# Three layer norms: half of the elementwise work moved from VectorE to ScalarE and GpSimd

## The reference, cut to what matters

```python
def _layer_norm(x, g, b):
    xf = x.astype(jnp.float32)
    mu = jnp.mean(xf, axis=-1, keepdims=True)
    var = jnp.mean(jnp.square(xf - mu), axis=-1, keepdims=True)
    y = (xf - mu) * lax.rsqrt(var + LN_EPS)
    return (y * g.astype(jnp.float32) + b.astype(jnp.float32)).astype(x.dtype)

x = first_block(x, ...)                     # ends with rms_norm(x, final_norm)
x = _layer_norm(x, ln_emb_g, ln_emb_b)      # norm 0
...                                         # proj = x @ w_in, attention, recurrence
x = _layer_norm(DEEPNORM_ALPHA * x + mix, ln_mix_g[l], ln_mix_b[l])   # norm 1
...                                         # up projection, convolution, gelu, down projection
x = _layer_norm(DEEPNORM_ALPHA * x + ffn, ln_ffn_g[l], ln_ffn_b[l])   # norm 2, the output
```

## Time and profile before

| | |
|---|---|
| median of 3 runs | 1375.38 us (1373.71 to 1377.1) |
| the profiled execution's own time | 1378.31 us |
| its span, first to last instruction | 1376.5 us |
| granted TensorE clock over the span | 0.98 |
| instructions | 19597 |

### The profile page before, as it was taken

One profiled execution on the slowest core, in us unless ns is written; L12 is line 12 of the kernel. 1 busy time (PEld: TensorE's weight loads), 2 busy tenths in 40 slices (PEclk: granted clock), 3 DMA queues, 4 the chain that ended last, 5 costly groups with the idle time before them and its releaser, 6 DMA issues.

```text
span 1376.5 us, 19597 instructions
## 1 busy us (share of the span) xinstructions
PE 1317.0 (96%) x7417; PEld 1143.1 (83%) x7417; DVE 954.6 (69%) x1272; ACT 729.9 (53%) x996; POOL 156.0 (11%) x136
## 2 busy tenths in 40 slices
PE   7999999699999999999999999999988999899996
PEld 6888887588888888888898888888888987788884
DVE  5766666868766676666667676666768678687777
ACT  6544456765444455444557755444454443465662
POOL 1200002258300000000025310000004110000000
PEclk9999999799999999999999999999998999999998
DMA  7755544046665546565454266555523343365650
GB/s 243 247 189 183 186 151 151 31 136 189 216 198 185 185 154 213 190 198 189 153 168 139 93 211 208 199 192 183 153 92 111 103 154 123 128 208 184 208 187 31
DMA packets 165425, 229.24 MB, mean 167 GB/s; under 512 B 4027, under 2 KB 135354, under 8 KB 165248
## 3 DMA queue, kind: packets, MB, share of 16 engines
q1 hardware_dynamic: 163120, 221.33, 49.3%
q0 software_dynamic: 2160, 7.24, 1.8%
q10 hardware_dynamic: 96, 0.02, 0.0%
HBM read 227.52 MB, written 1.05 MB: 166 GB/s over the span
## 4 chain that ended last, share of the span: by engine, by line
PE 83%; DVE 10%; ACT 3%; issue 2%; POOL 1%; DMA 0%; ACTq 0%; DVEq 0%
PE ps L425 28%; PE ps L432 15%; PE ps L371 12%; PE ps L372 11%; PE ps L373 11%; DVE w_lo L304 2%; POOL p_sb L1423 1%; PE ps L1336 1%; PE ps L639 1%; PE ps L2159 1%; ACT w_hi L296 1%; DVE h_both L675 1%; PE ps L1299 0%; DMA pt_sb<-in_ffn_norm_dram 0%; ACT h_both L658 0%
## 5 line engine op out<-in xcount | busy, mean ns | idle before, releaser
L304 DVE TENSOR_TENSOR w_lo<-raw,w_hi 128x2048 fp32r<-128x2048 f32 x208 | 479.8, 2308 | 110.8 <-ACT w_hi L296 110.7
L425 PE MATMUL ps<-h_both,w_hi 128*128 128x512 f32 x1760 | 424.9, 392 | 5.9 <-DVE h_both L770 2.9
L296 ACT ACTIVATE w_hi<-raw 128x2048 fp32r<-128x2048 f32 x208 | 396.5, 1908 | 15.4 <-PE ps L373 15.4
L425 PEld LDWEIGHTS ps<-h_both,w_hi 128*128 128x128 f32 x1760 | 326.4, 189 | 72.3 <-DVE w_lo L324 2.2
L432 PEld LDWEIGHTS ps<-h_both,w_lo 128*128 128x128 f32 x1760 | 228.3, 192 | 9.6
L432 PE MATMUL ps<-h_both,w_lo 128*128 128x256 f32 x1760 | 231.7, 283 | 0.0
L855 ACT ACTIVATE s_sb<-ps 128x512 f32<-128x512 f32 x88 | 52.5, 597 | 230.9 <-PE ps L432 230.9
L371 PE MATMUL ps<-w_hi,gu_hi 128*128 128x512 f32 x400 | 156.4, 391 | 0.8 <-DVE w_lo L304 0.8
L372 PE MATMUL ps<-w_hi,gu_lo 128*128 128x512 f32 x400 | 156.2, 391 | 0.0
L373 PE MATMUL ps<-w_lo,gu_hi 128*128 128x512 f32 x400 | 155.6, 389 | 0.0
L861 DVE TENSOR_TENSOR s_sb<-ps,s_sb 128x512 f32<-128x512 f32 x88 | 60.8, 690 | 103.4 <-ACT s_sb L855 103.4
(11 more groups left out here) (334 smaller groups left out, 1688.5 us busy)
## 6 DMA issues: line engine op xcount, KB each, us to landing
raw<-in_ffn_w_up_dram SPq DMA_DIRECT2D x44, 1024.0 KB, 5.3
raw<-in_ffn_w_down_dram SPq DMA_DIRECT2D x44, 1024.0 KB, 4.9
raw<-in_ffn_w_gate_dram SPq DMA_DIRECT2D x43, 1024.0 KB, 5.3
raw<-in_w_up_dram SPq DMA_DIRECT2D x22, 1024.0 KB, 5.0
raw<-in_w_in_dram SPq DMA_DIRECT2D x14, 1024.0 KB, 5.3
raw<-in_odd_w_qkv_dram SPq DMA_DIRECT2D x12, 1024.0 KB, 5.1
raw<-in_w_down_dram SPq DMA_DIRECT2D x11, 1024.0 KB, 4.9
raw<-in_even_w_in_dram SPq DMA_DIRECT2D x4, 1024.0 KB, 5.2
```

Of the source, the lines that this page charges most:

```text
L296: act.activation(w_hi[slot][:, :], raw[slot][:, :], ACT.Copy).then_inc(w_hi_ready, 1)
L304: dve.tensor_tensor(w_lo[slot][:, :], raw[slot][:, :], w_hi[slot][:, :].bitcast(F32), ALU.subtract).then_inc(w_lo_ready, 1)
L425: pe.matmul(PS[:, bank, :], a[:, k, t * P:(t + 1) * P], h_both[:, :, k, :], start=k == 0, stop=False, skip_group_check=True)
```

## The change

In all three layer norms the quarters of the upper feature half (quarters 2 and 3) lose VectorE's first instruction. In its place VectorE writes the negated mean to a new tile, neg_mean, right after the statistics are joined (`dve_mean`). ScalarE then adds neg_mean to each of the two upper quarters in place (`act_centre`), and GpSimd multiplies each by the weight row in place (`pool_gain`). VectorE takes the root meanwhile, does quarters 0 and 1 with its two instructions each as before, and for quarters 2 and 3 waits on the semaphore gained and does only the second instruction. In norm 0 the two engines work in XN and VectorE's second instruction reads XN.

The three semaphores for the arrival of the rows become one, vec_in, with waits for 48, 80 and 112. The transfers themselves and their order stay as they were.

```diff
--- before.py
+++ after.py
@@ -165,6 +165,7 @@
         gcol = sb("gcol", [P, 6 * KC])
         rs_tok = sb("rs_tok", [P, TB])
         rs_half = sb("rs_half", [P, TB])
+        neg_mean = sb("neg_mean", [P, TB])
         rs_wide = nc.alloc_sbuf_tensor_at("rs_wide", [P, S], F32, offset=place["fox_k_lo"])
         PS = ctx.enter_context(nc.psum_tensor("ps", [P, 8, 512], F32))
 
@@ -1828,6 +1829,28 @@
                 dve.bn_stats(bn[:, tb, half, :], X[:, tb, half * 512:(half + 1) * 512]).then_inc(stats_done, 1)
             return stats
 
+        mean_ready = sem("mean_ready")
+        centred = sem("centred")
+        gained = sem("gained")
+        upper = slice(512, 1024)
+
+        def dve_mean(dve):
+
+            dve.tensor_scalar(neg_mean[:, :], mv[:, :, 0], -1.0, None, ALU.mult).then_inc(mean_ready, 1)
+
+        def act_centre(act, at, z):
+
+            act.wait_ge(mean_ready, at + 1)
+            for tb in range(TB):
+                act.activation(z[:, tb, upper], z[:, tb, upper], ACT.Identity, bias=neg_mean[:, tb:tb + 1])\
+                   .then_inc(centred, 1)
+
+        def pool_gain(pool, at, z, g):
+
+            for tb in range(TB):
+                pool.wait_ge(centred, 2 * at + tb + 1)
+                pool.tensor_tensor(z[:, tb, upper], z[:, tb, upper], g[:, upper], ALU.mult).then_inc(gained, 1)
+
         def layer_norm(dve, at, g, b, rows_in, done, norm=None):
 
 
@@ -1835,13 +1858,17 @@
             for tb in range(TB):
                 m = dve.bn_aggr(mv[:, tb, :], bn[:, tb, :, :].rearrange("p a b -> p (a b)"))
             dlink(dve, m)
+            dve_mean(dve)
             dlink(dve, dve.tensor_scalar(ss[:, 0:2], mv[:, :, 1], EPS_LN, None, ALU.add))
             rsqrt(dve, ss[:, 0:2], 2)
-            dve.wait_ge(rows_in, 32)
+            dve.wait_ge(vec_in, rows_in)
             for tb, half in QUARTERS:
                 f = slice(half * 512, (half + 1) * 512)
                 x = X[:, tb, f]
-                dlink(dve, dve.scalar_tensor_tensor(x, x, mv[:, tb, 0:1], g[:, f], ALU.subtract, ALU.mult))
+                if half == 0:
+                    dlink(dve, dve.scalar_tensor_tensor(x, x, mv[:, tb, 0:1], g[:, f], ALU.subtract, ALU.mult))
+                else:
+                    dve.wait_ge(gained, 2 * at + tb + 1)
                 dve.scalar_tensor_tensor(x, x, ss[:, tb:tb + 1], b[:, f], ALU.mult, ALU.add).then_inc(done, 1)
                 if norm is not None and tb == 1:
                     norm.dve(dve, half=half)
@@ -1885,8 +1913,12 @@
                 for tb, half in QUARTERS:
                     f = slice(half * 512, (half + 1) * 512)
                     x = X[:, tb, f]
-                    dlink(dve, dve.scalar_tensor_tensor(x, XN[:, tb, f], mv[:, tb, 0:1], g[:, f], ALU.subtract, ALU.mult))
-                    dve.scalar_tensor_tensor(x, x, ss[:, tb:tb + 1], b[:, f], ALU.mult, ALU.add).then_inc(done, 1)
+                    if half == 0:
+                        dlink(dve, dve.scalar_tensor_tensor(x, XN[:, tb, f], mv[:, tb, 0:1], g[:, f], ALU.subtract, ALU.mult))
+                    else:
+                        dve.wait_ge(gained, tb + 1)
+                    z = x if half == 0 else XN[:, tb, f]
+                    dve.scalar_tensor_tensor(x, z, ss[:, tb:tb + 1], b[:, f], ALU.mult, ALU.add).then_inc(done, 1)
                     if tb == 1:
                         norm.dve(dve, half=half)
 
@@ -2443,8 +2475,6 @@
         bias_in = sem("bias_in")
         bias_masked = sem("bias_masked")
         vec_in = sem("vec_in")
-        vec2_in = sem("vec2_in")
-        vec3_in = sem("vec3_in")
         out_stored = sem("out_stored")
 
         g_rows_in = sem("g_rows_in")
@@ -2554,18 +2584,23 @@
 
             fox.pool_zero(pool)
             fox.pool_wf(pool)
+            pool.wait_ge(vec_in, 48)
+            pool_gain(pool, 0, XN, rowvec[:, 1, :])
             rec.pool(pool)
 
             pool.wait_ge(att_fox.scores, 8)
-            pool.dma_start(rowvec[:, 1, :], io["ln_mix_b_2"][0].partition_broadcast(P)).then_inc(vec2_in, 16)
+            pool.dma_start(rowvec[:, 1, :], io["ln_mix_b_2"][0].partition_broadcast(P)).then_inc(vec_in, 16)
             rec_out.pool(pool)
 
             pool.wait_ge(att_fox.out_ready, 8)
-            pool.dma_start(rowvec[:, 0, :], io["ln_mix_g_2"][0].partition_broadcast(P)).then_inc(vec2_in, 16)
+            pool.dma_start(rowvec[:, 0, :], io["ln_mix_g_2"][0].partition_broadcast(P)).then_inc(vec_in, 16)
+            pool.wait_ge(vec_in, 80)
+            pool_gain(pool, 1, X, rowvec[:, 0, :])
             pool.wait_ge(n_conv.normed, 3 * 4)
-            pool.dma_start(rowvec[:, 0, :], io["ln_ffn_g_2"][0].partition_broadcast(P)).then_inc(vec3_in, 16)
-            pool.dma_start(rowvec[:, 1, :], io["ln_ffn_b_2"][0].partition_broadcast(P)).then_inc(vec3_in, 16)
-            pool.wait_ge(vec3_in, 32)
+            pool.dma_start(rowvec[:, 0, :], io["ln_ffn_g_2"][0].partition_broadcast(P)).then_inc(vec_in, 16)
+            pool.dma_start(rowvec[:, 1, :], io["ln_ffn_b_2"][0].partition_broadcast(P)).then_inc(vec_in, 16)
+            pool.wait_ge(vec_in, 112)
+            pool_gain(pool, 2, X, rowvec[:, 0, :])
 
         @block.scalar
         def _(act):
@@ -2620,6 +2655,7 @@
             ffn2_1.act(act)
             fox.act_wf(act)
             final_norms.act(act)
+            act_centre(act, 0, XN)
             n_emb.act(act)
             for what, n in REC:
                 if what in ("unit", "second"):
@@ -2650,8 +2686,10 @@
                     n_gated.act(act, half=n)
                 elif what == "rec_proj":
                     rec_proj.act(act, n)
+            act_centre(act, 1, X)
             n_conv.act(act)
             conv_ffn.act(act)
+            act_centre(act, 2, X)
 
         @block.vector
         def _(dve):
@@ -2745,9 +2783,9 @@
                     n_gated.dve(dve, half=n)
                 elif what == "rec_proj":
                     rec_proj.dve(dve, n, stats_of(dve, mixed_x))
-            layer_norm(dve, 1, rowvec[:, 0, :], rowvec[:, 1, :], vec2_in, n_conv.normed, n_conv)
+            layer_norm(dve, 1, rowvec[:, 0, :], rowvec[:, 1, :], 80, n_conv.normed, n_conv)
             conv_ffn.dve(dve, stats_of(dve, conv_x))
-            layer_norm(dve, 2, rowvec[:, 0, :], rowvec[:, 1, :], vec3_in, out_x)
+            layer_norm(dve, 2, rowvec[:, 0, :], rowvec[:, 1, :], 112, out_x)
 
         @block.tensor
         def _(pe):
```

## The result

The changed kernel is slower: a median of 1384.8 us (1376.87 to 1386.69, five runs) against 1375.01 (1371.05 to 1377.1, five runs) for the kernel before, a ratio of 1.0061 with a 95% interval of 1.0039 to 1.0083. It was timed again twelve times beside 35 runs of before (e1_after_again): 1384.26 against 1375.49, ratio 1.0048 (1.0034 to 1.0063). The forecast was 1380.8, with a range to 1383.0.

The account below looks back on a forecast made before the run. TensorE, in flight for 96% of the span, was taken as the bound, norm work counting only where it waits. Norms of + 2.3, + 2.3 and + 0.8 made + 5.4 us on the median 1375.38: 1380.8 us, range 1377.0 to 1383.0.

Parts of the forecast that it names:

- VectorE stands until GpSimd's instruction is over.: Root in each norm: VectorE's small steps wait out GpSimd's two multiplies; 2.3 us a norm, bounds 0 and 2.8.
- (3): Rival, root in all norms: the tiny instructions slip past the two multiplies; - 1.2 us, 1374.2; chance 0.15.
- (5): Rival, on top of (3): earlier upper quarters speed TensorE in norms 0 and 1; - 4.3 us, 1371.1; chance 0.03.
- Norms 0 and 1 save nothing: Quarters 2 and 3 there have 1.4 us of slack ahead of TensorE, so dropping VectorE's first instructions brings nothing.
- the wait on gained never ends last: Norm 2: the multiplies end by 1369.63, and quarter 2 asks no sooner than 1371.11, so VectorE is not delayed.
- Norm 2.: Last norm: + 2.3 for the stopped root, - 1.56 saved, + 0.1 for store overlap, together + 0.8 us.
- The sum of the three norms.: Norm 0 + 2.3, norm 1 + 2.3, norm 2 + 0.8, together + 5.4 us; as the forecast, chance 0.50.
- In the sum I keep this cost as it is.: TensorE's restart: the half-rate stretch of 6.1 us, seen at norm 0, was taken to cost the same after the change.
- That execution lies 2.9 us above the median, so I put the difference on the median.: Whole kernel: + 5.4 was added to the median 1375.38, giving 1380.8, not to the profiled execution, which would give 1383.7.
- (2): Rival, restarts of norms 0 and 1: the clock returns at the same moment, giving 1.15 us back each; 1378.5; chance 0.20.
- (4): Rival, restarts: the slow stretch grows too, + 7.7 us, or the quarters also stand behind a late multiply; 1383.1; chance 0.12.

Follow-up runs that it names:

- e2: The changed kernel without GpSimd's multiplies, VectorE waiting on ScalarE's centring instead (part of the computation left out); 1372.86 us, ratio 0.998.
- e7: The changed kernel with only token block 0's upper quarter moved, so one GpSimd multiply a norm; 1379.68 us, ratio 1.0024.
- e8: The changed kernel with GpSimd clearing 1400 elements of a scratch tile in place of each multiply; 1369.52 us in one run.
- e10: The changed kernel with GpSimd's multiplies in norms 0 and 1 waiting until quarter 1 is written; 1374.90 us, ratio 1.0001.
- e12: The changed kernel with the root's products in PSUM and its estimate kept in both SBUF and PSUM; 1380.60 us, ratio 1.0039.
- e4: The kernel before plus eleven linked small VectorE steps ahead of the root in norms 0 and 1; 1382.46 us, ratio 1.0039.
- e5: The changed kernel with ten more filler matmuls ahead of the first turn in each of norms 0 and 1; 1381.36 us, ratio 1.0037.
- e14: The changed kernel with both the longer first fills of e5 and the seven fillers of e6; 1377.04 us, ratio 1.0014.
- e6: The kernel before plus seven filler matmuls around TensorE's turns in each of norms 0 and 1; 1371.16 us, ratio 0.9969.
- e11: The changed kernel with the root's scratch in PSUM, done column by column, eighteen small steps instead of nine; 1382.59 us, ratio 1.0065.

## Why the prediction was too low

- *VectorE stands until GpSimd's instruction is over.* Right. Taken as 2.3 us a norm; 2.09, 2.10 and 2.05 measured. Two long steps a norm, of 1.1 to 1.2 us, on the lines that it named (each one line further down in the new kernel). e2, e7, e8 and e10 show that it is the multiplies, that it goes by their number, and, with one run of e8 beside e12, that it takes two inputs of VectorE in SBUF and a GpSimd instruction that reads it. Rivals (3) and (5), with no stop, are out. The rows that it was read from were thinner than the text says: in the earlier trace rows the small steps start 0.68 and 0.66 us apart, not 0.65, and an addition takes 0.85 on the average.
- *Norms 0 and 1 save nothing; the wait on gained never ends last.* Right: both quarters 2 and 3 follow each other with no idle time (1005.04, 1.40 for the pair), and TensorE's restart moved by the delay of quarter 0 (0.18 us more in norm 1, from a turn at the lower clock).
- *Norm 2.* Forecast + 0.8, the trace shows + 0.6; of that the saving was 1.56 and measured 1.57.
- *The sum of the three norms.* Forecast + 5.4, the traces show + 4.8, and the means less the clock's part + 4.3.
- *"In the sum I keep this cost as it is."* This is the step that failed: the change in the clock's cost was put at nothing, and it measured + 3.8 us (an estimate, from 11 us more at the lower level). The rows that it rested on the earlier trace rows came from an execution in which the clock fell at both restarts, at norm 0 to a window mean of 0.89; kernels with an equally early restart read 0.94 and 1.00 in other executions. Held back by about 2 us, norm 0 reads 0.89 in all four profiles. e4 shows that a delay alone brings more time at the lower level (7.7 us, standard error 2.9), e5 that closing the gap undoes it on the average, e14 that with the clock held the loss is the fixed part.
- *"That execution lies 2.9 us above the median, so I put the difference on the median."* The same mistake once more. That execution had a mean clock of 0.980 against 0.9836 for the mean of 107, 10 us more at the lower level, which at 0.34 is 3.4 us and so all of the 2.9. The changed kernel has such a clock, or a lower one, in 13 of 17 runs. Added to its own execution the sum gave 1383.7, near the medians of 1384.8 and 1384.3, but by luck: nothing in the prediction said that the changed kernel would run at that execution's clock.
- *Rivals (2) and (4).* (2), that the clock gives part back, has the wrong sign. (4), that the slow stretch grows too, was right in kind and near in size, + 7.7 for a measured + 8.0 in the means; it had 0.12. The size is partly luck: it took 1.15 us of longer slow stretch at each restart, on top of a fall taken as given, where the runs show a fall that comes in more of the executions.

What is not settled: why the time at the lower level differs so much in the recurrence behind norm 0. Single profiles there read 0.94 to 1.00 (1020 to 1160 us) for late and early restarts alike. Of the 25 us at the lower level that lie between the two profiles of the changed kernel (mean clocks 0.987 and 0.978), about 14 are there (1.00 against 0.95) and 3 in the window of norm 1. So the restarts alone don't explain the spread of its runs, and one or two profiles for each kernel are too few to say whether a late restart bears on the recurrence.

## What to carry to other kernels

Before work is moved to GpSimd, list what VectorE runs in that time, and how much of it takes two inputs from SBUF: each GpSimd instruction that reads SBUF can hold up one such instruction for nearly its whole length, however small that one is (here 0.16 us of work, 1.1 to 1.2 us of standing). Put the moved work where the chain has slack (e10, which loses nothing but gains nothing either), not where the two engines seem to share the time best. And where TensorE's restart hangs on a chain of another engine, price a delay there by many runs with their granted clocks: a profile tells what one execution's clock did, and a few filler matmuls around the restart (e6) can be worth more than the change under study.

## What the runs showed of the hardware

- A VectorE step of 128 x 2 elements with two inputs in SBUF stood for 1.1 to 1.2 us under a GpSimd multiply of 1.25 us; the same step with one of the two in PSUM took 0.17 (e12), two steps of 128 x 1 that read PSUM alone took 0.36 together (e11), and a 128 x 512 one with an input in PSUM took its 0.69 (e10). Under GpSimd's clears all took 0.16 (e8). The Trainium skill, SBUF — State Buffer, section "Who interferes with whom", says this in full: one input in SBUF outside the two-port modes doesn't contend, two do, and only with a GpSimd instruction that reads. These runs agree on both kinds of input and on the reading. They didn't try a small step with a single input in SBUF and none in PSUM under a multiply; the one row of that kind, the start value L588 in the earlier trace rows, took 0.62 us under GpSimd's additions, and why is not shown.
- When the small steps slip past, the next instruction with two inputs in SBUF meets the rest of the multiply (e12's 1.64 us for 0.75).
- The same kernel's runs differ by up to 9 us (before, 1370.6 to 1379.8), in step with their mean granted clock of 0.989 to 0.980 (3.3 us for 10 us more at the lower level). Kernels whose restarts come about 2.1 us later spend 8 to 11 us more at the lower level (e4, after).
